# Dense gates by accumulating indirect DMAs in place of one-hot matmuls, and earlier V-row additions

## The reference, cut to what matters

```python
s1 = jnp.einsum('thd,hkd->thk', q1, keys_a); s2 = jnp.einsum('thd,hkd->thk', q2, keys_b)
v1, i1 = lax.top_k(s1, 16);  v2, i2 = lax.top_k(s2, 16)
...                                   # the 16 best of the pair sums
idx = jnp.take_along_axis(cand_i, pos, axis=-1)
gates = jax.nn.softmax(top_s, axis=-1)
u = expert_u[ib];  act = jax.nn.gelu(jnp.einsum('td,thkd->thk', hb, u))
vv = expert_v[ib]; return jnp.einsum('thk,thkd->td', gb * act, vv)
```

## Time and profile before

| | |
|---|---|
| median of 3 runs | 1668.12 us (1666.88 to 1669.82) |
| profiled execution, first to last instruction | 1668.3 us |
| mean granted clock of TensorE | 0.980 of 2.4 GHz |
| retrieval, from the first key load to the last turn | about 397 to 837 us |
| dense gates | about 837 to 1092 us |
| last U blocks, then V blocks | about 1092 to 1127, 1127 to 1654 us |
| DMA traffic | 426.84 MB, mean 256 GB/s |

### The profile page before, as it was taken

How to read it: one execution, slowest core, us unless ns; L and a number is a source line. 1 busy time by engine, 2 the same in 40 slices (tenths; PEclk the granted TensorE clock), 3 DMA queues, 4 the chain that set the end, 5 groups by cost and what they waited for, 6 DMA issues and landing times.

```text
span 1668.3 us, 23725 instructions
## 1 busy us (share of the span) xinstructions
PE 1590.2 (95%) x8101; PEld 1388.0 (83%) x8101; DVE 1281.9 (77%) x2618; ACT 722.5 (43%) x1188; POOL 422.3 (25%) x390
## 2 busy tenths in 40 slices
PE   5899899897899999999999999999999999999996
PEld 3787655676899999999999999998888888888885
DVE  6665333736858999999999999936888888888888
ACT  4223375326334343434367776734333333333333
POOL 0000133132423332332312222201333333333330
PEclk8999899998999999999999999999999999999998
DMA  8573300003668878878979899879999999999992
GB/s 319 211 286 119 126 1 1 1 26 136 222 214 270 276 235 287 288 246 257 322 235 324 303 330 316 320 271 314 339 352 359 350 356 351 362 350 358 350 354 98
DMA packets 176964, 426.84 MB, mean 256 GB/s; under 512 B 15168, under 2 KB 99280, under 8 KB 172112
## 3 DMA queue, kind: packets, MB, share of 16 engines
q1 hardware_dynamic: 139984, 291.14, 49.8%
q0 software_dynamic: 36864, 134.23, 23.3%
HBM read 372.88 MB, written 52.43 MB: 255 GB/s over the span
## 4 chain that ended last, share of the span: by engine, by line
PE 71%; DVE 1%; issue 0%; ACT 0%; DVEq 0%; ACTq 0%
PE ps_y L1874 10%; PE ps_y L1878 10%; PE ps_y L1876 10%; PE ps_u L1091 10%; PE ps_u L1092 10%; PE ps_u L1093 10%; PE ps_g L1586 5%; PE ps_q L1273 1%; PE ps_q L1275 1%; PE ps_q L1274 1%; PE ps_s L1285 1%; DVE y_scaled L1849 0%; DVE row L1856 0%; PE ps_u L1898 0%; DVE y_row L1170 0%
## 5 line engine op out<-in xcount | busy, mean ns | idle before, releaser
L1091 PE MATMUL ps_u<-h_hi,u_hi 128*128 128x384 f32 x1024 | 349.4, 341 | 1.7 <-DVE u_lo L1081 1.7
L1093 PE MATMUL ps_u<-h_hi,u_lo 128*128 128x384 f32 x1024 | 345.1, 337 | 0.0
L1092 PE MATMUL ps_u<-h_lo,u_hi 128*128 128x384 f32 x1024 | 345.0, 337 | 0.0
L1150 POOL DMA_INDIRECT row<-in_v,row_index x128 | 176.4, 1378 | 401.9 <-DVE y_row L1170 306.3
L1753 ACT CAST v_hi<-v_raw 128x1024 fp32r<-128x1024 f32 x128 | 134.7, 1053 | 327.4 <-issue 327.4
L1150 POOL DMA_INDIRECT row<-in_u_rows,row_index x128 | 151.1, 1181 | 451.1 <-DVE row_dots L1157 381.5
L1810 DVE TENSOR_TENSOR v_lo<-v_raw,v_hi 128x1024 fp32r<-128x1024 f32 x128 | 160.7, 1255 | 103.1 <-ACT v_hi L1753 103.1
L1874 PE MATMUL ps_y<-v_hi,w_hi 128*128 128x512 f32 x768 | 237.5, 390 | 0.0
L1878 PE MATMUL ps_y<-v_hi,w_lo 128*128 128x512 f32 x768 | 236.5, 389 | 0.0
L1876 PE MATMUL ps_y<-v_lo,w_hi 128*128 128x512 f32 x768 | 236.5, 389 | 0.0
L1081 DVE TENSOR_TENSOR u_lo<-u_raw,u_hi 128x1024 fp32r<-128x1024 f32 x128 | 166.9, 1310 | 79.7 <-ACT u_hi L1074 79.6
(11 more groups left out here) (275 smaller groups left out, 2369.1 us busy)
## 6 DMA issues: line engine op xcount, KB each, us to landing
u_raw<-in_u SPq DMA_DIRECT2D x128, 512.0 KB, 5.0
v_raw<-in_v SPq DMA_DIRECT2D x128, 512.0 KB, 6.2
w_ada<-in_w_ada SPq DMA_DIRECT2D x24, 1024.0 KB, 6.6
activations<-u_act SPq DMA_DIRECT2D x128, 192.0 KB, 5.2
gate_tiles<-g_tile SPq DMA_DIRECT2D x12, 2048.0 KB, 9.2
gates<-gate_tiles SPq DMA_DIRECT2D x32, 768.0 KB, 9.0
act<-activations SPq DMA_DIRECT2D x128, 192.0 KB, 6.4
w_proj<-in_w_proj SPq DMA_DIRECT2D x16, 512.0 KB, 4.0
```

Source lines behind the costliest of these rows:

```text
L1091: pe.matmul(out, self.hi[n][:, k], hi, start=(k == 0), stop=False)
L1092: pe.matmul(out, self.hi[n][:, k], lo, start=False, stop=False)
L1093: last = pe.matmul(out, self.lo[n][:, k], hi, start=False, stop=(k == KD - 1))
L1150: pool.indirect_dma_start(out=self.row[n][:], out_offset=None, in_=self.table[q // PICKS], in_offset=bass.IndirectOffsetOnAxis(ap=self.ind ...
```

## The change

The dense gate matrix becomes a flat DRAM tensor `dense_gates` of 16384 x 384 floats, expert by expert. In `stick_breaking` SP zeroes it with 32 stores from a zeroed tile (POOL makes that first in its list). In each retrieval turn DVE also computes, for the 384 tokens, the place of each pick (expert times 384 plus token), and POOL issues indirect DMAs that add a column of 128 gates (one for each partition's token, 4 B each) at those places. There are 3 x 128 = 384 of them: 36 in each of the turns 2 to 7, 168 in the stage after, spread before the gathers of each. The first scatter of a head and token tile waits until all earlier heads' scatters of that tile have landed. The stage `dense_gates` goes; `up_only` keeps its U blocks, dots and gathers. In `experts`, SP waits for all 384 scatters before the first of its gate loads, which are now one for each block, from a ring of four. The V-row additions begin at U block 122, and their accumulators have memory of their own, so the wait for the last product goes.

```diff
+SCATTERS = DENSE_TILES * PICKS
 TURN_START = [0, 6, 16, 26, 36, 46, 56, 66, 80]
 DOTS_BY = [0, 0, 8, 20, 32, 44, 56, 68, 81]
-GATED = 120
+SCATTERED_BY = [0, 0, 0, 36, 72, 108, 144, 180, 216]
+TAIL_U = 120
+ZERO = 1536
+ZEROED = 16 * (N_KEYS * DENSE // ZERO)
...
+            sp.wait_ge(zeros_made, 1)
+            for n in range(N_KEYS * DENSE // ZERO):
+                sp.dma_start(g_dram[n * P * ZERO:(n + 1) * P * ZERO].rearrange("(p z) o -> p (z o)", p=P), zero[:])\
+                  .then_inc(g_zeroed, 16)
+            sp.wait_ge(g_zeroed, ZEROED)
...
+            pool.memset(zero[:], 0.0).then_inc(zeros_made, 1)
             operands.constants(pool)
...
+    def scatter(self, pool, s, g_dram, g_zeroed):
+        h, b, k = s // (DENSE_TILES * TOPK), s // TOPK % DENSE_TILES, s % TOPK
+        j = h * TOPK + k
+        if s == 0:
+            pool.wait_ge(g_zeroed, ZEROED)
+        pool.wait_ge(self.placed, h + 1)
+        pool.wait_ge(self.gated, h + 1)
+        if h > 0 and k == 0:
+            pool.wait_ge(self.scattered[b], 16 * TOPK * h)
+        pool.indirect_dma_start(out=g_dram, out_offset=bass.IndirectOffsetOnAxis(ap=self.place[:, b, j:j + 1], axis=0),
+                                in_=self.gate[:, 1 + b, j:j + 1], in_offset=None, compute_op=ALU.add)\
+            .then_inc(self.scattered[b], 16)
...
-                for r in range(gathered(h), gathered(h + 1)):
-                    rows.gather(pool, r)
+                gather_and_scatter(pool, rows, g_dram, g_zeroed, range(gathered(h), gathered(h + 1)),
+                                   range(SCATTERED_BY[h], SCATTERED_BY[h + 1]))
...
-                note(dve.tensor_copy(expert[:, :, h * TOPK:(h + 1) * TOPK], picked[:]))
-                dve.wait_ge(chain, steps[0])
+                dve.scalar_tensor_tensor(rows.place[:, :, h * TOPK:(h + 1) * TOPK], picked[:, 1:TB], float(DENSE),
+                                         rows.base[:].broadcast_to([P, DENSE_TILES, TOPK]), ALU.mult, ALU.add).then_inc(rows.placed, 1)
...
-def dense_gates(nc, life, keep, picks, up, rows, h_row, g_dram, g_stored):
...
+def gather_and_scatter(pool, rows, g_dram, g_zeroed, gathers, scatters):
+    n = max(1, len(gathers))
+    for q in range(n):
+        for s in scatters[q * len(scatters) // n:(q + 1) * len(scatters) // n]:
+            rows.scatter(pool, s, g_dram, g_zeroed)
+        for r in gathers[q:q + 1]:
+            rows.gather(pool, r)
...
+def up_only(up, rows, h_row, g_dram, g_zeroed):
+    def gpsimd(pool):
+        gather_and_scatter(pool, rows, g_dram, g_zeroed, range(gathered(PEER_HEADS), PICKS + rows.RING),
+                           range(SCATTERED_BY[PEER_HEADS], SCATTERS))
+    def vector(dve):
+        for b in range(FIRST, TAIL_U):
+            up.vector_at(dve, b)
+            for r in dots_at(b):
+                rows.dot(dve, r, h_row)
...
-        FIRST_ADD = 1
+        FIRST_ADD = 2 - OPENING
...
+                if i == 2 - OPENING:
+                    sp.wait_ge(rows.row_used, PICKS)
+                    for n in range(3):
+                        load_act(n)
+                        load_v(n)
+                    load_act(3)
+                if i == 5 - OPENING:
+                    for b in range(DENSE_TILES):
+                        sp.wait_ge(rows.scattered[b], 16 * PICKS)
+                    for n in range(3):
+                        load_gates(n)
...
-                if i == FIRST_ADD:
-                    dve.wait_ge(up.mul, N_KEYS)
```

## The result

The changed kernel takes 2053.11 us (median of 4 runs, 2049.49 to 2061.2) against 1668.53 us for the kernel before in the same comparison: a ratio of 1.2308, 95% interval 1.2279 to 1.2337. It is 385 us slower. The sign was forecast and the time lies in the range (1700 to 2090), but it is 150 us above the predicted 1903 and above the stretch of 1780 to 2019 us that the forecast itself had. The profiled execution has a span of 2059.0 us.

A forecast was written before the change was run, and what follows sets the result against it. PE bounds the kernel before; POOL's list of scatters and gathers then takes over, delaying the V products from 1127 to 1361 us. 1668.3 + 234 + 1 (memset) - 0.6 (additions) gives 1903 us; range 1700 to 2090 us (0.8).

The forecast's parts named there:

- What bounds it, before and after: Whole kernel: PE bounds it before (busy 1590.2 of 1668.3 us); after, POOL's list does, done at 1346 us.
- Rival A: POOL: scatters are cheap to issue, PE stays the bound, 1580 us; faster at all below 1.13 us per scatter; chance 0.08.
- The price of an issue: POOL: a scatter costs what a 128-index gather does, 0.94 us plus 0.30 until the next, 1.24 us; 476 us for 384.
- sign of being wrong: Wrong if scatters take much less or more than 0.94 us, PE never waits before V, or landings hold up POOL.
- The stalls: POOL issues wait for DVE instructions with two SBUF inputs, 230 u_lo and dots: 156 to 225 us, taken as 190.
- rival C: POOL stalls as in the burst (1.85 us each, 2019 us) or issues cost 0.47 us more (2083 us); chance 0.08.
- Who waits: Retrieval and U blocks: PE waits for w_query_lo some 30 us a turn, turns take 84 us, dots wait for rows.
- Behind POOL: Between POOL's end and the first V product: scatter landing 6 us, gate load 6, weighing and splits 3, together 15 us.
- Zeroing hidden: The 32 zeroing stores behind w_out end at 280 us, hidden; 35 us at a slower pace, 0 taken.
- The additions: V-row additions seven blocks earlier free the second residual at the end: some 0.6 us gained.
- Rival D: DMA engines are the bound, from about 1 us of each engine per scatter: 2108 us or more; chance 0.10.
- Rival B: POOL is the bound but hardly stalls, since starved DVE leaves gaps: 1712 us; up to 1780 has chance 0.12.

The follow-up runs named there:

- e2: The changed kernel with plain indirect writes in place of accumulating ones, same number of DMAs and elements: 1848.44 us, ratio 1.1062 to the kernel before.
- e4: The changed kernel with the 128 dot products of the row tokens each replaced by a small memset: 2001.17 us, ratio 1.1981 to the kernel before.
- e8: The changed kernel with the low halves of the query weights made on VectorE and not on POOL: 2020.66 us, ratio 1.2100 to the kernel before.
- e7: The changed kernel with all 384 scatters issued after the retrieval, between the last gathers: 2189.77 us in one run.
- e3: The changed kernel with each scatter replaced by an indirect gather of 128 elements of 4 B from the gate matrix: 1838.75 us in one run.
- e10: The changed kernel without scatters and with the V-row additions at their old place, from the second V block on: 1584.21 us, against 1584.52 without that move.
- e1: The changed kernel without its 384 scatters and their waits, gate loads and zeroing kept: 1584.52 us, ratio 0.9493 to the kernel before.

## Why the prediction was right, and where its sizes were off

**What bounds it, before and after: right.** POOL's list replaced PE. Rival A (cheap scatters, 1580 us) fell: its condition was 1.13 us per scatter with all stalls, and (1508.0 - 509.9 - 156 - 23.8) / 384 = 2.13 was measured. That the time goes with the list is shown by e2 (price), e4 (stalls), e8 (24 us of other work in it) and e7 (its start).

**The price of an issue: mis-sized, and the largest error.** "I take the same price" (1.24 us) failed; 1.86 was measured, 238 us over 384 scatters. The bound beside it, "half as much again ... if an accumulating element ... costs POOL a third transfer", gave 1.71 and was the right idea, still 0.15 short. The prediction's own sign of being wrong (a scatter that takes much more than 0.94 us) came true. I took the row with the same count of addresses and had no row at all for the addition. e3 shows that the first half of the reasoning holds (4 B or 4 KB, in or out, 0.94 to 0.97 us), e2 that the addition is the rest.

**The stalls: right kind, half the size.** 190 us forecast, 104 found. The step "nearly each of these 230 catches one start, and on average half of it is left" gives 0.6 us and more per DVE instruction; the trace has 104 / 230 = 0.45. In e2, at the price that I had assumed, POOL took 1297.9 - 510.5 = 787 us for a list of 384 x 1.27 + 120 x 1.28 + 24 = 665: 122 us of stalls, 0.53 each. So even with the assumed price my sum (1903) was 55 us above e2's 1848. Why less than half an instruction is lost was not tried by itself. In e7, where DVE mostly waits, it is 22 us over 93 such instructions, 0.24 each.

**The two errors have opposite signs,** 238 up and 86 down; the later start (3 us), the gathers (7) and the end behind POOL (-6) make up the 156 us between 1361 and 1517. That the time lies in the range is in part luck: with the right price and the stalls as forecast the sum gives 1903 + 238 = 2141 us, outside it. The measured 2053 lies where rival C was (2019 to 2083), which had 0.08, and not in the forecast's 0.60.

**Who waits: right.** PE's wait at query_of is 169.3 / 4 = 42 us a turn (forecast 30), the turn is some 100 us (query_low begins at 509.9, 612.9, 710.4 and 810.4; forecast 84, which with 36 x 0.62 = 22 us more for the price would be 106), dots wait for rows. The V stage runs at its old pace.

**Behind POOL: 9.4 us for 15.** The landings were taken from medians over a busy stretch and counted from POOL's end. But a landing is counted from the start of the issue: the last scatter landed 2.98 us after its start and 1.4 us after POOL's end. The load of gates took 4.19 us, against 6.

**Zeroing hidden: right.** Stores of 768 KB landed in 20.9 us, side by side, and the block's end moved from 288.75 to 291.07, 2.3 us, of which 1.87 had come before the block began. The additions: nothing to be measured, e10.

**Rival D (DMA engines): out.** Queue 0 took 26.9% of 2059.0 us after and 24.6% of 1582.2 in e1: 165 us of each engine for 384 scatters, 0.43 us each, where 1 us was needed. **Rival B** (hardly any stalls, 1712 us) fell with them: 104 us. **Rival C** is the one that came, in its second form, a dearer issue, and with fewer stalls than it had.
The Trainium skill, DMA: Bandwidth & Descriptors, section "Anatomy of one DMA - SWDGE (gpsimd) path", calls descriptor generation "small, variable". The trace shows POOL's whole time for an issue and not its parts: 0.94 us for 128 elements and 1.56 with an addition, which set the end of this kernel, and the measurement decides.

## What to carry to other kernels

An indirect DMA has a price per issue on POOL that does not fall with the bytes, and an addition raises it by more than half; count issues times pitch before you ask what TensorE saves. Find the engine whose list is full (busy tenths at a ceiling, gaps of constant length) rather than the largest wait: taking away a wait of 169 us gave 32. And half-used engines that feed each other have less room than their busy share says: a third of the scatters fitted POOL's total and still cost 19 us. (That the small ring of eight rows is a reason was not tried.) Last, look at what an ordering wait stands behind when you reorder a list: with one tile alone POOL waited for its own scatters to land, 16 to 30 us in three of the kernels.

## What was not expected of the hardware

- Packets: a plain indirect DMA of 128 elements of 4 B is 32 packets on the software queue, an accumulating one 144, as many as a gather of 128 rows of 4 KB.
- Landing of an accumulating scatter, from the start of its issue: 2.9 us at the least and 3.1 at the median in e7, where little else moved. The issue itself is 1.55 us of that.
- The same 7324 PE records are 1506.4 us of busy time in e1 (granted clock 0.98) and 1582.5 after (0.889). The 76 us are not on the path: POOL's list sets the end, and PE waits in between.
